# Expert weights of a diffusion trunk step: another order of the eleven slot loads of an expert

## The reference

```python
def moe_ffn(h, router, w_gu, w_down):           # w_gu (8, 1024, 2816), w_down (8, 1408, 1024)
    logits = (h @ router).astype(jnp.float32)
    top_v, top_i = lax.top_k(logits, TOP_K)     # TOP_K = 2
    w = jax.nn.softmax(top_v, axis=-1)
    combine = jnp.sum(jax.nn.one_hot(top_i, N_EXPERTS) * w[..., None], axis=-2)
    g, u = jnp.split(jnp.einsum('btd,edf->btef', h, w_gu), 2, axis=-1)
    act = jax.nn.silu(g) * u * combine[..., None]
    return jnp.einsum('btef,efd->btd', act, w_down)
```

## Time and profile before

| | |
|---|---|
| median of 3 runs | 2366.56 us (2366.43 to 2367.58) |
| the profiled execution, its own time | 2363.55 us |
| its span, first to last instruction | 2361.7 us |
| TensorE busy | 2241.4 us, 95% of the span |
| granted TensorE clock, mean | 0.972 |
| HBM read, written | 537.64 MB, 14.93 MB |
| expert layers | about 787 to 1181 us and 1961 to 2355 us |

### The profile page before, as it was taken

The page is one execution under the profiler, slowest core; times in us unless marked ns, Lnnn a source line. Parts: engine busy times, 40 slices in busy tenths (PEclk is TensorE's granted clock), DMA queues, the critical chain, the costliest instruction groups (busy, mean ns, idle before and its releaser), DMA issues.

```text
span 2361.7 us, 43842 instructions
## 1 busy us (share of the span) xinstructions
PE 2241.4 (95%) x19531; PEld 1614.3 (68%) x19531; DVE 483.8 (20%) x1376; ACT 393.0 (17%) x819; POOL 66.9 (3%) x109
## 2 busy tenths in 40 slices
PE   6999998999999999899998899999998889998999
PEld 4776666888888655445676588888878875454455
DVE  2234332000112400000211410002344423000002
ACT  1133223000100100000113310002143331000001
POOL 4000001000000000000000000000000000000000
PEclk8999999999999899999999899999999999999999
DMA  8967898753356499999574695414440057999991
GB/s 326 275 232 286 314 318 268 210 155 116 107 169 210 151 384 387 380 379 382 211 241 170 225 277 177 134 36 125 132 136 7 12 178 256 386 382 379 379 387 51
DMA packets 355909, 550.90 MB, mean 233 GB/s; under 512 B 11280, under 2 KB 311184, under 8 KB 343232
## 3 DMA queue, kind: packets, MB, share of 16 engines
q1 hardware_dynamic: 344352, 525.31, 64.1%
q0 software_dynamic: 5840, 18.11, 3.0%
q10 hardware_dynamic: 5536, 4.73, 0.6%
HBM read 537.64 MB, written 14.93 MB: 234 GB/s over the span
## 4 chain that ended last, share of the span: by engine, by line
PE 85%; DVE 5%; DMA 3%; SPq 3%; ACT 2%; issue 1%; ACTq 0%; DVEq 0%
PE ps L641 83%; SPq L481 3%; DMA ring<-in_moe_w_down 2%; ACT ring L1441 1%; DVE ring L1989 1%; ACT work L1441 1%; DVE ring L2007 0%; DVE work L1848 0%; PE ps L1137 0%; DVE ring L2012 0%; DVE ring L1997 0%; PE ps L1032 0%; DMA ring<-in_ada_w 0%; DVE ring L2015 0%; PE ps L667 0%
## 5 line engine op out<-in xcount | busy, mean ns | idle before, releaser
L641 PE MATMUL ps<-ring,work 128*32 128x384 f32 (+6 forms) x7752 | 700.7, 452 | 36.7 <-DMA ring<-in_moe_w_down 26.0
L641 PE MATMUL ps<-hT,ring 128*128 128x256 f32 x3200 | 714.6, 382 | 3.4 <-DVE hT L1858 3.2
L641 PEld LDWEIGHTS ps<-hT,ring 128*128 128x128 f32 x3200 | 609.4, 191 | 113.3 <-issue 12.2
L641 PEld LDWEIGHTS ps<-ring,work 128*32 128x32 f32 (+2 forms) x7752 | 340.5, 116 | 371.7 <-issue 257.0
L1441 ACT ACTIVATE work<-ps 128x256 f32<-128x256 f32 (+5 forms) x244 | 101.8, 436 | 1350.7 <-PE ps L641 1170.5
L641 PE MATMUL ps<-work,ring 128*128 128x256 f32 (+1 forms) x1344 | 289.7, 375 | 10.9 <-DVE work L2074 6.3
L641 PEld LDWEIGHTS ps<-work,ring 128*128 128x128 f32 (+1 forms) x1344 | 243.0, 188 | 47.3 <-DVE work L2074 8.0
L641 PE MATMUL ps<-ring 64*64 64x64 f32 (+1 forms) x4192 | 183.2, 230 | 18.6 <-ACT ring L1441 7.2
L641 PEld LDWEIGHTS ps<-ring 64*64 64x64 f32 x4192 | 160.7, 139 | 58.0 <-ACT ring L1441 24.2
L1441 ACT ACTIVATE ring<-ps 128x512 f32<-128x512 f32 (+3 forms) x208 | 101.6, 491 | 341.0 <-PE ps L641 329.9
L641 PE MATMUL ps<-work 128*128 128x128 f32 (+2 forms) x736 | 107.4, 297 | 4.3 <-DVE work L2194 4.2
(11 more groups left out here) (263 smaller groups left out, 948.9 us busy)
## 6 DMA issues: line engine op xcount, KB each, us to landing
ring<-in_moe_w_gu SPq DMA_DIRECT2D x96, 1536.0 KB, 16.0
ring<-in_ada_w SPq DMA_DIRECT2D x96, 1024.0 KB, 7.1
ring<-in_moe_w_down SPq DMA_DIRECT2D x48, 1536.0 KB, 16.1
ring<-in_ff_w_gu SPq DMA_DIRECT2D x88, 512.0 KB, 6.0
ring<-in_dn_w_in SPq DMA_DIRECT2D x32, 1024.0 KB, 5.4
ring<-in_moe_w_gu SPq DMA_DIRECT2D x32, 1024.0 KB, 8.8
ring<-in_ff_w_down SPq DMA_DIRECT2D x44, 512.0 KB, 7.3
ring<-in_moe_w_down SPq DMA_DIRECT2D x32, 512.0 KB, 11.6
```

The costliest lines, as they stand in the source:

```text
L641: return pe.matmul(out, lhsT, rhs, start=start, stop=stop, **kw)
```

## The change

The tuple that sets the order in SP's loop is another:

```diff
                     with sp.Fori(0, n_more) as r:
                         e = sp.value_load(order_e[0:1, bass.ds(r + 1, 1)], min_val=0, max_val=NE - 1)
-                        for j in (0, 1, 4, 5, 2, 3, 6, 7, 8, 9, 10):
+                        for j in (0, 1, 4, 5, 6, 2, 8, 3, 7, 9, 10):
                             if j in GU_FREE:
                                 sp.wait_ge(moe["p_gu"], (done[0] + r) * 6 + GU_FREE[j])
```

## The result

The changed kernel takes 2384.72 us (median of 4 runs, 2384.0 to 2394.15) against 2366.49 us (median of 4, the three of the table above and one more): a ratio of 1.009, 95% interval 1.0068 to 1.0113. It is slower, by 18.2 us in the medians. The profiled execution took 2394.15 us.

The account below looks back on a forecast made before the run. Expert layers begin paced by TensorE, then by the weights from the third or fourth expert. Shifts of 6.1 to 7.5 and 6.4 to 8.0 us, taken as 14, gave span 2375.7, median 2380.5 us; 8-in-10 range 2372 to 2393.

Parts of the forecast that it names:

- the two waits of each body: TensorE waits about 5 us ahead of gate(0) for slot 2, then about 3 us ahead of up(0) for slot 3.
- from pair to pair: Expert layers: up(0) to next up(0) takes 93.5 to 94.1 us, shrinking the shift to 6.1 to 7.5 us in layer 1.
- a distance above 94.5: Sign in the new trace: bodies further apart than 94.5 us would speak for a second clock fall or a longer-dry queue.
- main case: Slots 2 and 3 land late for the bodies, costing 12.5 to 15.5 us in all; chance 0.70.
- Places of slots 2 and 3: Bodies: in a never-empty queue one place later lands 4.2 us later, two places 8.4 us, not hidden.
- The first shift: First delay of up(0) in each layer: 8.5 us at expert 2, 8.8 us at expert 10.
- rival (4): Queue runs dry longer than 1 us because slot 8 holds back 3 and 7; 2 us more gives 2388; chance 0.11.
- The slow clock: Bodies: the low clock after the first wait falls into the second wait, so it costs nothing more.
- rival (3): Clock falls again in the wait for slot 3; six bodies cost 15 us more, 2395; chance 0.10.
- (2): Not slower: slots 6 and 8 ahead keep the queue fed across down(0), giving 2353 us; chance 0.04.
- (5): No difference, since slot 3's part of the body is covered somewhere: 2366 us; chance 0.05.
- What I had called hidden: Slot 7 one place later for up(2), and slot 3 for small experts' up(2) with 13 us of cover, cost nothing.

Follow-up runs that it names:

- the kernel with slot 8 last: Against the changed kernel, slot 8 goes back behind 3 and 7 in rounds beside a body; new order kept beside small experts; ratio 1.0023 to the kernel before.
- the kernel of 2351.83 us: Against the kernel before, rounds beside small experts load slots in order 0 to 10, rounds beside bodies keep the old order; 2351.83 us, ratio 0.9954.

## Why the prediction came out as it did

The direction, the two waits of each body and the range came as predicted: slower, 2372 to 2393 predicted, 2384.72 measured. The point was 4.2 us too low by the medians, and 9 us too low by the layers (14 against 23.0). The step that failed is the one from pair to pair: the prediction had up(0) come 93.5 to 94.1 us after the last, and it comes 95.4 to 95.7 after it. The prediction had named a distance above 94.5 as a sign against its main case, and the sign is there. The wide expert shows the same: its mark, counted from the layer's own start, is 11.8 us late in layer 1, and not 6 to 8. That the time still fell into the main case's own range, 2374 to 2387, is partly luck: 23.0 us on the base of 2366.56 would have been 2389.6.

Two sums of the working are off as well. 8.5 less the 2.2 us between 189.2 and 187.0 is 6.3, not 6.1, and 8.8 less 2.0 is 6.8, not 6.4; the sum then runs from 13.1 to 15.5 us, which leaves 14 about where it was.

**Places of slots 2 and 3.** Right, though the two waits were shared out otherwise: 6.1 to 7.5 and 0.5 to 0.8 us, not 5 and 3. In the trace of after, the down rows of slot 3 for expert 2 are issued at 877.3 and land 13.9 us later, at 891.2; up(0) starts at 891.3. The row of expert 4 reads the same, 972.6 + 13.9 = 986.5 and a start at 986.7:

```profile
L485 SPq DMA_DIRECT2D ring<-in_moe_w_down x1: 5826/5826/5826, 877.3 to 877.3; - x1
...
  PE ps L641: 0.8, 1
...
DMA to landing us min/median/max: 13.9/13.9/13.9
```

With the order changed for the bodies alone this gave 8.5 us of layer length.

**The first shift.** Predicted 8.5 us in layer 1 and 8.8 in layer 3. Counted from the layer's own start it is 891.32 - 2.76 - 878.3 = 10.3 and 2081.80 - 19.93 - 2052.9 = 9.0. The missing 1.8 us of layer 1 are in the landing of slot 8 during the first body, taken as 6.3 us from issue. It took 8.9, and landed 838.1 us after the start by the clock of before, not 835.9:

```profile
L485 SPq DMA_DIRECT2D ring<-in_moe_w_down x1: 372/372/372, 832.0 to 832.0; - x1
...
DMA to landing us min/median/max: 8.9/8.9/8.9
```

The queue was idle then: from 828 to 832 the engines moved 2 GB/s. The second trace of the changed kernel has 8.6 us here; why it is more than 6.3 no run shows. In layer 3 the same load took 7.0, beside the later bodies 6.4 to 7.8. A lone transfer in the idle queue of the earlier trace rows was near the lower end of this, not its value.

**The step that was mis-sized: from pair to pair.** The prediction had the loop (up(0), down(1), slot 8, twelve slots, the next up(0)), and its first part was right: 43.2 us from up(0) to the landing of slot 8, measured 928.3 + 6.6 - 891.3 = 43.6. But it then said that the queue "just runs dry, for about 1 us", and took 50.3 to 50.9 us for the twelve slots behind, so that a pair came to 93.5 to 94.1 and the shift shrank. A pair takes 95.4: from the landing of slot 8 to that of slot 3 it is 51.6 (934.9 to 986.5). The stretches around slot 8's issue show the hole:

```profile
921.00:925.00 4.00, 4.00 (x48) 2.91 (x46) 0.61 (x2) 1.06 (x2) 0.00 (x0) 1.00 1.08 363
925.00:929.00 4.00, 4.00 (x69) 2.56 (x59) 0.00 (x0) 0.43 (x1) 0.00 (x0) 1.00 0.41 148
929.00:933.00 4.00, 4.00 (x65) 2.85 (x67) 0.69 (x1) 0.03 (x1) 0.00 (x0) 1.00 0.90 296
933.00:937.00 4.00, 4.00 (x80) 2.36 (x76) 0.00 (x0) 0.00 (x0) 0.00 (x0) 1.00 1.07 376
...
1020.00:1024.00 4.00, 4.00 (x70) 2.45 (x63) 0.00 (x0) 0.12 (x2) 0.00 (x0) 1.00 0.70 244
1024.00:1028.00 4.00, 4.00 (x60) 2.97 (x62) 0.69 (x1) 0.39 (x1) 0.00 (x0) 1.00 0.77 256
```

At 148 and 296 GB/s instead of some 376, the transfers of (1 - 148/376) x 4 + (1 - 296/376) x 4 = 3.3 us are missing, and 2.7 in the next pair. The kernel before has no such hole behind a body: 365 to 370 GB/s in the same place. TensorE is busy in all these stretches; the hole costs it nothing there, and everything at the next body. That is the mean over 16 engines. What a pair pays is read better from landings, here those of slot 2 and slot 8, first beside a small expert, where the queue is full, then beside the body of expert 2:

```profile
L485 SPq DMA_DIRECT2D ring<-in_moe_w_down x1: 3966/3966/3966, 871.3 to 871.3; - x1
...
DMA to landing us min/median/max: 11.9/11.9/11.9
...
L485 SPq DMA_DIRECT2D ring<-in_moe_w_down x1: 373/373/373, 875.5 to 875.5; - x1
...
DMA to landing us min/median/max: 11.6/11.6/11.6
...
L485 SPq DMA_DIRECT2D ring<-in_moe_w_down x1: 3262/3262/3262, 917.4 to 917.4; - x1
...
DMA to landing us min/median/max: 11.3/11.3/11.3
...
L485 SPq DMA_DIRECT2D ring<-in_moe_w_down x1: 372/372/372, 928.3 to 928.3; - x1
...
DMA to landing us min/median/max: 6.6/6.6/6.6
```

In the full queue slot 8 lands 3.9 us behind slot 2 (883.2 and 887.1), beside the body 6.2 us behind it (928.7 and 934.9). The hole costs slot 8 some 2.3 us, and the pair has grown by 2.1 (95.4 - 93.3). In the other three pairs slot 8 lands 5.8, 7.1 and 6.2 us behind slot 2. So the prediction had the landing of slot 8 nearly right and made the full queue that it compared it with too slow: such a queue would have landed slot 8 at 928.7 + 3.9 - 891.3 = 41.3 us after up(0), and not at 41.9 to 42.4.

The twelve slots behind were taken as too short for another reason. In layer 1 one landing interval of each pair is long, in the kernel before too: there slot 2 of expert 3 lands 5.3 us behind slot 5. In the changed kernel it falls behind slot 8 (5.3 us for slot 7 of expert 3, 5.6 for slot 3 of expert 5). An average of 4.24 us over 22 slots spreads it over the pair; the twelve intervals that contain it are 51.6 and 51.9 us. It is no second hole, since the engines move 385 and 400 GB/s in the two stretches from 937 to 945; what makes it long is open. Where slot 8's own interval is 7.1 us, in the first pair of layer 3, no long one follows and the twelve take 50.8.

The low rate ahead of slot 8's issue has a likely reason: the first of the 16 engines have already run out of work while the last still finishes slot 2. Slot 2's down rows land at 928.7, slot 8 is issued at 928.3, and between 925 and 929 the engines already move only 148 GB/s. That this spread of the engines is the reason is my reading of these rows; no run isolates it.

The four pairs take 381.9 us together; with the middle of my range, 93.8, they would take 375.2. So the sum grows by 6.7 us; with the 1.8 us of the first shift and 0.2 of layer 3's it is 14 + 8.7 = 22.7, against 23.0 measured.

That this is the closed loop and not a price of slot 8's wait by itself was shown from three sides: slot 8 in front without bodies that wait for slot 3, 3.4 us; late bodies without slot 8 in front, 8.5 and 5.5 us; both, 23.0. And with slot 3 moved ahead of 8, the same stretch of the trace is nearly full:

```profile
915.00:919.00 4.00, 4.00 (x73) 2.24 (x72) 0.00 (x0) 0.60 (x1) 0.00 (x0) 1.00 1.08 368
919.00:923.00 4.00, 4.00 (x55) 3.21 (x55) 0.69 (x1) 0.46 (x1) 0.00 (x0) 1.00 0.93 335
923.00:927.00 4.00, 4.00 (x84) 2.38 (x76) 0.00 (x0) 0.00 (x0) 0.00 (x0) 1.00 1.03 398
```

So rival (4), with a chance of 0.11, was true in substance and the main case, with 0.70, was not: the queue ran dry for about 3 us by its rate and 2.3 by slot 8's landing, not 1. I had priced 2 us more at 8 us; what the pairs lost was 6.7.

**The slow clock.** Chosen as free, and it was: it lies between the two waits. The stretch from 880.2 us has the lower clock, and gate(0) takes 7.17 us in it; the wait for slot 3 is correspondingly 0.8 and not 3 us:

```profile
880.20:887.00 6.80, 3.68 (x26) 1.84 (x29) 0.00 (x0) 0.00 (x0) 0.00 (x0) 0.50 1.05 386
887.00:892.00 5.00, 4.18 (x52) 1.84 (x50) 0.00 (x0) 0.55 (x2) 0.00 (x0) 1.00 1.05 377
```

Behind the second wait the 192 records take 15.68 us in each body, so the clock does not fall again, and rival (3) is out for this kernel. The rule of the Trainium skill (TensorE: Matmul & The Clock Gate, HAM oscillation), in the form in which I had applied it to both waits, does not hold here: the long wait was followed by the lower clock, the short one was not. In the kernel before the same loss lay behind the only wait, on the path. And what rival (3) feared does happen where the first wait is the short one, as in the first body that waits in the kernel with slot 8 last:

```profile
878.49 5.36 PE L645 MATMUL ps<-ring,work 128*32 128x384 f32 x64 [1.89 <-DMA ring<-in_moe_w_down]
887.10 17.37 PE L645 MATMUL ps<-ring,work 128*32 128x384 f32 x192 [3.25 <-DMA ring<-in_moe_w_down]
```

There gate(0) takes 5.36 us, and the 192 records behind the second wait take 17.37 us in place of 15.68; the mean granted clock is 0.60 from 887 to 891. The length of a wait alone does not tell: in the kernel of 2351.83 us a wait of 3.92 us was followed by 22.16 us for the 256 records of the four pieces, and one of 3.83 us by 20.84, the time at full clock.

**Rivals (2) and (5)** are out: nothing was gained from feeding the queue, and slot 3 was not covered. What I had called hidden was hidden: no small expert waits for slot 3 or 7, and from up(0) of expert 6 to the mark in the wide expert it is 1150.73 - 1082.03 = 68.7 us, as before (1136.15 - 1067.5).

**By the medians** the kernel lost 18 to 20 us and not 23. That it is 18 here and 20 the second time is the base: the kernel before had a median of 2366.49 over 4 runs, and of 2362.9 to 2363.8 in the three later series of 15 to 32 runs; the changed kernel's two medians are 1.3 us apart. In both traces of the changed kernel the layers hold about 23; the rest is outside them and is not settled.

## What to carry to other kernels

In a queue that is always full each place back is one transfer later, so the order in which the consumer wants the buffers decides, and the order in which they come free only as far as the queue would otherwise run out of work; here the first was worth 12 us and the second cost 18. Before a load that has to wait is moved forward, look at what the queue still holds at that moment: a wait that is harmless while the consumer is early (3 us here) empties the queue when the consumer is late, and every round then makes the next one later, here by 2.1 to 2.4 us a pair. To price the hole, compare the late landing with that of a full queue read from the same slot, and not with an average interval: 6.2 against 3.9 us here, where the average is 4.24.

## What was unexpected of the hardware

A load issued as the queue ran out landed 5.8 to 7.1 us behind the one ahead of it, where the same slot takes 3.9 us in a full queue. The mean rate of the 16 engines had fallen to 148 GB/s in the 4 us ahead of such an issue, while the slot ahead was still landing. Slot 8's 1536 KB took 6.3 us from issue to landing alone, 6.4 to 7.8 beside seven of the eight bodies of the changed kernel, and 8.9 beside the first of layer 1, although the queue was idle when it was issued.
